# Two edits at once around the gated delta rule: its front in another order, and its doubling levels as 64x64 products, with the modulation sums moved to other stages

## The reference

```python
diff = gcum[..., :, None] - gcum[..., None, :]
decay = jnp.where(causal, jnp.exp(jnp.where(causal, diff, 0.0)), 0.0)
k_beta = k * beta[..., None]
m = jnp.where(strict, jnp.einsum("bhnid,bhnjd->bhnij", k_beta, k) * decay, 0.0)
uw = lax.linalg.triangular_solve(m + eye, rhs, left_side=True, lower=True, unit_diagonal=True)
...
attn_qk = jnp.einsum("bhnid,bhnjd->bhnij", q, k) * decay
...
mod = (c_act @ w_mod + b_mod)[:, None, :]
mod_c = (cc_act @ w_mod + b_mod)[None, None, :]
```

## Time and profile before

| | us |
|---|---|
| median of 3 runs (1073.87 to 1075.74) | 1074.66 |
| the profiled execution, its own time | 1073.88 |
| its span | 1072.0 |
| PE busy | 1019.6 (95%) |
| DVE busy | 854.2 (80%) |
| ACT busy | 603.9 (56%) |
| POOL busy | 97.8 (9%) |

### The profile page before, as it was taken

One profiled execution on the slowest core, in us unless ns is written; L12 is line 12 of the kernel. 1 busy time (PEld: TensorE's weight loads), 2 busy tenths in 40 slices (PEclk: granted clock), 3 DMA queues, 4 the chain that ended last, 5 costly groups with the idle time before them and its releaser, 6 DMA issues.

```text
span 1072.0 us, 20308 instructions
## 1 busy us (share of the span) xinstructions
PE 1019.6 (95%) x7444; PEld 938.4 (88%) x7444; DVE 854.2 (80%) x1528; ACT 603.9 (56%) x1039; POOL 97.8 (9%) x115
## 2 busy tenths in 40 slices
PE   6998998999999999999999999999999879999995
PEld 6997898999999889888999998888767679998884
DVE  5898898988889879775898889768787875557765
ACT  5798424566666555475766666455444545445543
POOL 1014232000000100000100001002000210000001
PEclk9999999999999999999999999999999999999998
DMA  9774242567775878636776667734321056766871
GB/s 288 186 232 128 83 145 80 181 196 213 220 214 194 298 212 260 232 99 223 213 215 194 195 195 272 251 90 154 100 78 59 20 146 188 195 198 221 272 232 40
DMA packets 216256, 193.28 MB, mean 180 GB/s; under 512 B 6032, under 2 KB 193568, under 8 KB 216064
## 3 DMA queue, kind: packets, MB, share of 16 engines
q1 hardware_dynamic: 206560, 158.09, 49.2%
q0 software_dynamic: 9200, 33.73, 9.4%
q10 hardware_dynamic: 432, 0.61, 0.2%
HBM read 191.35 MB, written 1.06 MB: 179 GB/s over the span
## 4 chain that ended last, share of the span: by engine, by line
PE 76%; DVE 12%; ACT 5%; issue 4%; DMA 2%; POOL 0%; POOLq 0%; ACTq 0%; DVEq 0%
PE ps L598 23%; PE ps L600 22%; PE ps L599 22%; DVE cv L2120 2%; DVE wL L2098 2%; DMA raw<-in_a_w_in 1%; ACT wH L1292 1%; PE ps L768 1%; PE ps L1114 1%; PE ps L814 1%; DVE cv L2889 1%; PE ps L1092 1%; PE ps L900 1%; ACT p_b L1569 0%; PE ps L965 0%
## 5 line engine op out<-in xcount | busy, mean ns | idle before, releaser
L1292 ACT ACTIVATE wH<-raw 128x1024 fp32r<-128x1024 f32 x298 | 311.3, 1060 | 226.9 <-PE ps L600 205.7
L2098 DVE TENSOR_TENSOR wL<-raw,wH 128x1024 fp32r<-128x1024 f32 x298 | 356.3, 1221 | 71.2 <-ACT wH L1292 69.6
L598 PE MATMUL ps<-yH,wH 128*128 128x256 f32 x704 | 195.0, 277 | 0.0
L600 PE MATMUL ps<-yH,wL 128*128 128x256 f32 x704 | 194.4, 276 | 0.0
L599 PE MATMUL ps<-yL,wH 128*128 128x256 f32 x704 | 194.4, 276 | 0.0
L598 PE MATMUL ps<-xH,wH 128*128 128x256 f32 x512 | 142.2, 278 | 3.4 <-DVE xL L2098 1.6
L599 PE MATMUL ps<-xL,wH 128*128 128x256 f32 x512 | 141.4, 276 | 0.0
L600 PE MATMUL ps<-xH,wL 128*128 128x256 f32 x512 | 141.4, 276 | 0.0
L599 PEld LDWEIGHTS ps<-yL,wH 128*128 128x128 f32 x704 | 132.2, 188 | 0.1
L598 PEld LDWEIGHTS ps<-yH,wH 128*128 128x128 f32 x704 | 132.2, 188 | 0.1
L600 PEld LDWEIGHTS ps<-yH,wL 128*128 128x128 f32 x704 | 132.2, 188 | 0.0
(11 more groups left out here) (422 smaller groups left out, 1915.8 us busy)
## 6 DMA issues: line engine op xcount, KB each, us to landing
raw<-in_f_w_up SPq DMA_DIRECT2D x88, 512.0 KB, 4.8
raw<-in_w_ff SPq DMA_DIRECT2D x64, 512.0 KB, 4.4
modw<-in_w_mod_t POOLq DMA_DIRECT2D x48, 512.0 KB, 4.9
raw<-in_f_w_down SPq DMA_DIRECT2D x44, 512.0 KB, 4.6
raw<-in_a_w_in SPq DMA_DIRECT2D x32, 512.0 KB, 4.9
raw<-in_w_in SPq DMA_DIRECT2D x22, 512.0 KB, 4.1
raw<-in_w_kv SPq DMA_DIRECT2D x16, 512.0 KB, 5.1
raw<-in_a_w_out SPq DMA_DIRECT2D x8, 512.0 KB, 4.0
```

What stands on the lines that cost most here:

```text
L598: mm(o, l[0], r[0], start=first, stop=False, skip_group_check=check)
L600: return mm(o, l[1], r[0], start=False, stop=last, skip_group_check=check)
L1292: fn(slot(wH, c), raw[:, c % RAW], ACT.Copy).then_inc(hi_done, 1)
L2098: return tt(o, x, hi.bitcast(F32), ALU.subtract)
```

## The change

In PE's stream `gate_sums` now forms the row sums itself with 16 broadcast products into banks 4 to 7, in front of the last qkv block (`row_diagonals` and `dG` are gone); the key products come in front of z(0). DVE does the four differences and arguments right after the gate sums, and the convolution of block 11 behind the four systems. POOL adds the upper mask in one go, later. The levels use only the 64x64 diagonal blocks: 32 products of 64 rows, 64 weight columns and 32 moving columns take the place of 16 of 128 by 128 by 64, each half of the partitions into a PSUM bank of its own, in two steps of 8 matrices instead of four of 4. Of the modulation sums 4 instead of 12 stand in the levels, 5 instead of 6 in the scan behind them and 3 instead of 5 ahead of wo_a; down0 has 13 instead of 11, the q blocks 8 instead of 5, and 6 new ones stand ahead of and in wo_b. The loads of three units of wo_a (`lo`) go behind the levels.

```diff
                 pe.wait_ge(g_dve, 4)
+                pe.wait_ge(bank_free, BANK["qkv"] + 9)
                 for t in range(TT):
-                    mm(ps[7][:, 8 * t:8 * t + 8], K_["tri"], sm[:, 10, 8 * t:8 * t + 8], start=True, stop=True)
-                mm(ps[7][:, 16:24], K_["ones"], sm[:, 10, 0:8], start=True, stop=True).then_inc(g_sum, 1)
+                    mm(ps[0][:, 8 * t:8 * t + 8], K_["tri"], sm[:, 10, 8 * t:8 * t + 8], start=True, stop=True)
+                mm(ps[0][:, 16:24], K_["ones"], sm[:, 10, 0:8], start=True, stop=True).then_inc(g_sum, 1)
+                for g in range(4):
+                    for x in range(4):
+                        n = 4 * g + x
+                        last = mm(ps[AUX + g][:, x * P:(x + 1) * P], sm[:, 10, n:n + 1].broadcast_to([P, P]), K_["tri"],
+                                  start=True, stop=True)
+                    last.then_inc(row_pe, 1)
...
-                    row(g)
-                z(0)
+                pe.wait_ge(silu_done, 8)
                 for g in range(4):
                     pe.wait_ge(diff_dve, g + 1)
                     products(g, 8).then_inc(kk_pe, 1)
+                pe.wait_ge(g_dve, 5)
+                z(0)
                 z(1)
-                turns_of((0, 1))
+                turns_of(range(4))
                 z(2)
-                turns_of((2, 3))
                 pe.wait_ge(silu_done, 12)
...
+                def tile_products(a, lhs, rhs, c):
+
+                    for x in range(8 * a, 8 * a + 8):
+                        for f, r in enumerate(HALVES):
+                            i = rhs(r, x)
+                            o = ps[AUX + 2 * a + f][r, c + x % 8 * 32:c + x % 8 * 32 + 32]
+                            if len(i.shape) == 3:
+                                o = o.rearrange("p (n s) -> p n s", s=i.shape[2])
+                            last = mm(o, lhs[r, x, r], i, start=True, stop=True)
+                    last.then_inc(dbl_pe, 1)
+
+                def corner_products(a, bank, out, k, lhs, rhs):
+
+                    for x in range(8 * a, 8 * a + 8):
+                        o = ps[bank + a][out, x % 8 * 64:x % 8 * 64 + 64]
+                        last = mm(o, lhs[k, x, out] if lhs is MT else lhs[k, x, 0:64], rhs[k, x, k], start=True, stop=True)
+                    last.then_inc(dbl_pe, 1)
...
                 for e, l in enumerate(LEVELS):
                     final = l == LEVELS[-1]
-                    for g in range(4):
-
-                        pe.wait_ge(dbl_dve, 8 * e + g + 1)
+                    for a in range(2):
                         if e == 0:
+                            pe.wait_ge(at_dve, 2 * a + 2)
+                        if final:
+                            corner_products(a, AUX, HALVES[1], HALVES[0], MT, T_)
+                        else:
+                            tile_products(a, MT, lambda r, x: halves(T_[r, x, r], l, 0), 0)
...
-            for o, x, n in ((tok[:, 0, 16:24], vb[:, 0:8], 4), (tok[:, 1, 16:24], vb[:, 8:16], 6)):
+            for o, x in ((tok[:, 0, 16:24], vb[:, 0:8]), (tok[:, 1, 16:24], vb[:, 8:16])):
                 ptt(o, o, wide(x, HK), ALU.mult).then_inc(scan_pool, 1)
             pool.wait_ge(bank_free, BANK["z"] + 4)
+            pool.wait_ge(at_dve, 4)
...
                 dve.wait_ge(g_sum, 1)
-                st.do(nc.vector.tensor_copy(sm[:, 16, 0:16], ps[7][:, 0:16]))
-                tt(sm[:, 18, 0:8], ps[7][:, 16:24], sm[:, 16, 0:8], ALU.subtract).then_inc(g_dve, 1)
+                st.do(nc.vector.tensor_copy(sm[:, 16, 0:16], ps[0][:, 0:16]))
+                tt(sm[:, 18, 0:8], ps[0][:, 16:24], sm[:, 16, 0:8], ALU.subtract).then_inc(g_dve, 1)
+                for g in range(4):
+                    q4 = slice(4 * g, 4 * g + 4)
+                    dve.wait_ge(row_pe, g + 1)
+                    tt(AT[:, q4], four(ps[AUX + g][:]), bc(gc[:, q4], P), ALU.subtract).then_inc(diff_dve, 1)
+                    dve.wait_ge(diff_dve, g + 1)
+                    tt(U_[:, q4], rep(K_["low"], 4), AT[:, q4], ALU.subtract).then_inc(arg_dve, 1)
 
...
+                j = BLOCKS["qkv"][1] - 1
+                lo(0, 8, U("qkv") + 2 * j + SPLIT)
                 key_sums(0)
                 system(0)
                 system(1)
-                lo(0, 8, U("z") + SPLIT + 1)
+                lo(0, 8, U("qkv") + 2 * j + SPLIT + 1)
                 key_sums(1)
                 system(2)
                 system(3)
-                small(0)
-                small(1)
+                free("qkv", 0, j)
+                convolve(j)
+                lo(0, 8, U("z") + SPLIT)
+                lo(0, 8, U("z") + SPLIT + 1)
+                for g in range(4):
+                    small(g)
                 lo(0, 8, U("z") + SPLIT + 2)
-                small(2)
-                small(3)
...
 
...
+                    for a in range(2):
+                        x8 = slice(8 * a, 8 * a + 8)
+                        dve.wait_ge(dbl_pe, 4 * e + a + 1)
                         if final:
-                            tt(P_[:, q4], four(ps[AUX + g][:]), rep(join[:, e], 4), ALU.mult).then_inc(dbl_dve, 1)
+                            r = HALVES[1]
+                            last = ts(P_[r, x8, 0:64], eight(ps[AUX + a][r, :]), -1.0, None, ALU.mult)
-                    if not final:
-                        mod_sums(2)
-                    for g in range(4):
-                        tt(o, o, packed(g), ALU.add).then_inc(dbl_dve, 1)
-                    if not final:
-                        mod_sums(2)
+                            for f, r in enumerate(HALVES):
+                                last = tt(P_[r, x8, 0:32], eight(ps[AUX + 2 * a + f][r, 0:256]), rep(join[r, e], 8), ALU.mult)
+                        last.then_inc(dbl_dve, 1)
+                    mod_sums(1)
...
                 nbe = sm[:, 20, 0:8]
+                lo(0, 8, U("z") + 5 + SPLIT)
+                ahead(0, U("z") + 6)
+                mod_sums(2)
-                mod_sums(2)
+                mod_sums(3)
...
-            mod_sums(5)
+            mod_sums(3)
...
-            blocks("q", query_tiles, after=lambda j: mod_sums(1 if j else 2))
+            blocks("q", query_tiles, after=lambda j: mod_sums(2))
             values_and_band()
-            modulation()
-            added("wo_b", "f1", lambda k: col("f_norm1", k))
+            mod_sums(3)
+            added("wo_b", "f1", lambda k: col("f_norm1", k), after=lambda j: mod_sums((2, 1, 0, 0)[j]))
```

More of the change, by code:

```diff
@@ L87 @@
 MOD_LATE = 30
-MODS_WITH = {"down0": (1, 3, 4, 5, 7, 9, 10, 11, 13, 15, 17), "down1": (0, 1, 3, 5, 7, 9, 11, 13, 15, 17), "ff2": range(2, 18, 2)}
+MODS_WITH = {"down0": (1, 3, 4, 5, 6, 7, 9, 10, 11, 12, 13, 15, 17), "down1": (0, 1, 3, 5, 7, 9, 11, 13, 15, 17), "ff2": range(2, 18, 2)}
 def mod_products(tile):
@@ L109 @@
 _c = 0
-for _name, _count in (("ident", P), ("ones", P), ("tri", P), ("low", P), ("upT", P), ("join", 4 * P),
+for _name, _count in (("ident", P), ("ones", P), ("tri", P), ("low", P), ("upT", P), ("join", 96),
                       ("band8", 16), ("eye8", 8), ("neg7", 1)):
@@ L157 @@
 OUT_BANK = ((2, 3), (6, 7))
+HALVES = (slice(0, 64), slice(64, 128))
 DECAYS = (2, 3, 0, 1)
@@ L327, in build @@
         P_ = feat[:, 16:24, :].rearrange("p a (b c) -> p (a b) c", b=2)
-        dG = [zs[:, g // 2, (g % 2) * 512:(g % 2 + 1) * 512].rearrange("p (a b) -> p a b", a=4) for g in range(4)]
         modw2, = place(80.1875, ("modw2", [P, MOD_RING, D]))
@@ L801, in delta_front_pe @@
             def delta_front_pe():
-                def row(g):
-                    pe.wait_ge(dg_act, g + 1)
-                    if g == 3:
-                        pe.wait_ge(g_dve, 5)
-                    mm(ps[AUX + g][:], K_["ones"], dG[g].rearrange("p a b -> p (a b)"),
-                       start=True, stop=True).then_inc(row_pe, 1)
                 def products(g, f0):
@@ L1793, in silu_a @@
                 fn(feat[:, bass.ds((i * 4 + j) * 2, 2)], cv[:, n % 2], ACT.Silu).then_inc(silu_done, 1)
-            def row_diagonals(g):
-                act.wait_ge(g_dve, 4)
-                for x in range(4):
-                    n = 4 * g + x
-                    last = fn(dG[g][:, x], K_["tri"], ACT.Copy, scale=sm[:, 10, n:n + 1])
-                last.then_inc(dg_act, 1)
             def input_block(j):
@@ L1984, in _ @@
             ptt(sel.rearrange("p k (b j) -> p k b j", j=8), x, x, ALU.mult).then_inc(sel_pool, 1)
-            for g in range(4):
-                part = slice(4 * g, 4 * g + 4)
-                pool.wait_ge(arg_dve, g + 1)
-                ptt(AT[:, part], AT[:, part], four_of(cst[:, CONSTS["upT"][0]:CONSTS["upT"][0] + P]), ALU.add).then_inc(arg_pool, 1)
             for g in range(4):
@@ L2411, in delta_front, with eight @@
                     tt(AT[:, q4], four(ps[AUX + g][:]), AT[:, q4], ALU.mult).then_inc(at_dve, 1)
-                lo(0, 8, U("z") + 5 + SPLIT)
-                ahead(0, U("z") + 6)
             def delta():
```

(28 more changed lines are left out.)

123 lines of the change are left out of this document (53 added, 70 removed).

## The result

On one chip the kernel before took 1075.32 us (median of 19 runs) and the changed one 1068.25 (19 runs, 1063.87 to 1074.39), a ratio of 0.9934 with a 95% interval of 0.9922 to 0.9946: 7.1 us less, where 9.9 less was forecast (1064.0 is 10.7 below the median of 1074.66, as the sum was taken from a profiled execution 0.8 under it). The time lies in the stated range of 1058.5 to 1072.5, but just above the forecast's own of 1059.6 to 1067.7. The profiled execution of the changed kernel had a span of 1066.4, against 1072.0, so it shows 5.6 of the 7.1.

What follows compares the result with a forecast made beforehand. PE, 95% busy, was taken as the bound. Front 1.0, levels 12.1, scan -0.3, wo_a 0.6 and band -3.5 sum to 9.9 off the profiled 1073.88: 1064.0 us, range 1058.5 to 1072.5, the forecast's own 1059.6 to 1067.7.

Steps and rivals of the forecast that it cites:

- The levels, gain 12.1: Four doubling levels: 64x64 tiles overlap, a group of 32 instructions costs 1.0 us, levels take 24.1 instead of 36.2.
- The rival of partial overlap: Levels: tiles overlap only in part, a group of 32 costs 1.55 us, gain 4.9 instead of 12.1; time 1071.2, chance 0.16.
- the serial one: Levels: products stay serial, 64 instructions take 3.7 us, so the change does nothing; time 1074.2, chance 0.12.
- The gain hangs on the moved sums: Levels: with the old four modulation sums each, DVE would need 7.7 us a level and be the bound.
- Front, +1.0: Front up to `kq`: row sums on PE and DVE's new order start it 1.0 us earlier, bounds +3.2 and -0.2.
- The second stall of the inverse: Inverse on DVE: POOL's second back-to-back product also falls on it and slows another small operation, -1.15 us.
- The statement that DVE, not ACT, would end the waits: Front: turned systems and `small_rows` come 2 us earlier, with DVE instead of ACT ending PE's waits.
- Scan, -0.3: Scan behind the levels: one modulation sum goes but three `lo` come, about 0.3 us lost.
- wo_a, +0.6: Ahead of wo_a: two modulation sums leave, where PE waited 0.57 for a `lo`; 0.6 us gained.
- Band, -3.5: q blocks and band: one more sum 1.2 and three blocks late by 0.75 each, 3.5 us lost; bounds -1.3, -6.
- the sign that was forecast: Band: the first turn waits some 4 to 5 us, with a tile of `modw` ending DVE's idle time.
- The rival of the slow clock: Levels: PE's clock falls to half, 22 us of work become 44; time 1087, slower than before, chance 0.05.

Runs made afterwards that it cites:

- the tile order: The changed kernel with each group's products ordered as eight of the upper half, then eight of the lower, instead of alternating: 1084.42 us, ratio 1.0089.
- the old sums: The changed kernel with all modulation sums where they stood in the kernel before: 1076.82 us, ratio 1.0010.
- the front alone: The kernel before with only the new front put in, levels, sums and POOL's fetches as they were: 1073.30 us, ratio 0.9978.
- the tok order: The changed kernel with ACT copying `tok` ahead of the two weight copies and POOL multiplying `tok` behind the query products: 1065.13 us, ratio 0.9908.

## Why the prediction was right, and what it missed

- **The levels, gain 12.1**: measured 12.2 (24.0 instead of 36.2). A group of 32 instructions cost 1.00 as taken; the tile order shows that this is overlap, at 1.61 a group without it where the bound was 1.85. The rival of partial overlap and the serial one fell. Of the Trainium skill ("TensorEngine Tiling (Array Packing)", Key Properties) the parallel tiles hold here. A drain at the change of mode is not visible: a turn starts 2.0 after its product. Its Instruction Overhead puts about 60 cycles on each product, by 2.4 GHz an estimate of 0.025, and the 0.031 per instruction lie above that, so no run here contradicts it as a floor. But 32 columns were not as dear as 64: on one tile they took 0.050, where the 64 columns of the last level, all on one tile, took 0.063 (149.78 to 151.80 for 32).
- **The gain hangs on the moved sums**: shown, and more strongly than forecast: with the old sums 1.2 of the 12.2 was left, the fall of the clock included. One term was too small: DVE's eight operations on 64 partitions took 3.6 a level (1.75 and 1.82), not 2.8, as 0.35 had been taken from operations on 128 partitions. With one sum a level that still fits into 6.0.
- **Front, +1.0**: 1.9. The argument (line 2341) took 0.69, where the trace of before had 1.28 to 1.45 beside POOL's additions; that gave DVE 2.5 us that the walk did not count. 1.6 of them went again into two small operations beside POOL's additions (0.98 and 0.97 instead of 0.17, at 91.39 and 92.65), and two waits came that it had not either: `small` stood 2.61 behind POOL, and `small_rows` 1.90 behind `tok`. The second stall of the inverse came as forecast (0.94 and 1.55). The statement that DVE, not ACT, would end the waits was wrong: ACT's `tok`, with the two weight copies ahead of it, ended the longest.
- **Scan, -0.3**: -1.4. This term was mis-sized: the three `lo` and the five sums behind them made DVE late, and moving two sums out gave 1.3 back. That the `lo` took 5.20 and not 3 x 1.2 is POOL's product on `tok` beside the second (153.66, 2.02); in the kernel before it stood beside a sum (2.79 instead of 1.23), so that part is not new.
- **wo_a, +0.6**: +0.9.
- **Band, -3.5**: -3.5 to the third scores, but the agreement is in part luck: five other traces with the same q blocks and band have 17.2 to 17.8 there instead of 18.4, a loss of 2.3 to 2.9. The term had three q blocks late by 0.75 each for PE, and that did not happen (scores at the same 11.4 us lead); what came late was DVE. The maxima came 7.0 behind the first scores instead of 4.1, and these 2.9 are what the wait has grown by: 1.2 is the sum ahead of them, and 1.5 is the last evacuation of q, late behind a second sum that had waited 1.32 for its tile (430.19), the sign that was forecast. The last 0.6 is low clock. When the last sum was gone 1.3 to 1.8 stayed, and with all sums in their old places nothing.
- **What the sum did not have** is the clock outside the levels. In the profiled execution the first block of wo_a took 15.0 instead of 12.5, with 6.8 us of low clock around the wait of 2.66 (in windows of 0.2 us, 172.8 to 179.8), and the last stage lost 1.8, with 10.2 us of low clock instead of 3.4. These 4.3 are the distance between the 9.9 forecast and the 5.6 in the profile. They are no fixed price of the change: behind the same wait ahead of wo_a the first block took 12.0 and 12.2 in two traces of kernels with the changed levels, and 13.9 in the front alone, where the scan is the old one; the last stage, the same program in all, took 190.4 to 196.0. By the medians 2.8 are missing. That some of it is the change's the clocks of all executions show: the mean granted clock was 0.983 to 0.991 in the 19 of the changed kernel (median 0.988) and had a median of 0.992 in the kernel before on each of the three chips of the experiments. 0.004 of 1068 us is 4 us, an estimate, as not all of it is on the path. Where the low stretches lie and how long they are is a matter of the single execution. The changed kernel's 19 times spread over 10.5 us and those of the kernel before over 4.8, but on another chip 30 of the kernel before spread over 9.1.
- **The rival of the slow clock** was given 0.05 and did not occur in the changed kernel itself (1.00 over the 24 us). It did occur in the run with the same tile order, behind the waits for DVE in the one with the old sums, and behind a wait of only 0.73 in the one with the tok order. Its mechanism was nearer than I had rated it.

## What to carry to other kernels

Block-diagonal products on half the rows and columns pay best when neighbouring instructions name different tiles (here 1.0 us for 32 instead of 1.6), and only if the engines that follow them have the time; move their side work before counting the gain. Side work moved elsewhere has a price at each new place: here none seen in down0, about its own 1.2 us ahead of the band's maxima, and 4.4 or more in wo_b, where it waits for transfers (low clock behind the new wait included). Count for each new wait of PE not only its length but the half clock that may follow it, and look for waits first where PE's work is sparse. A stretch of low clock in one trace is not yet a cost of the change: look for it in a second trace of the same kernel.

## What the runs showed of the hardware

- Products of 64 rows, 64 weight columns and 32 moving columns started 0.031 us apart on alternating tiles and 0.050 on the same one.
- The clock was granted at 0.60 over 34 us in which PE was busy without a gap, with such products on one tile at a time and turns between them; with alternating tiles it stayed at 1.00 over 24 us.
- A wait of 0.73 between such products was followed by 6.8 us of low clock in four of four kernels; 3.6 us of useless products in a wait of 4.2 kept it at 1.00.
- The same program with the same waits had low clock of different length around them (6.8 and 3.4 us around 2.66), and around 2.60 in a near kernel none. What decides it stays open.
- Beside POOL's products of about 1.9 us on `tok`, DVE operations with two inputs in SBUF took up to 1.6 us more (0.25 to 1.55, 1.23 to 2.78), but those that read PSUM took no longer (1.75 for four of 64x256, 1.83 elsewhere).
